# Raw projections, a shorter choice of experts and weights in halves at the layer ends of a two-layer encoder

## What is computed

```python
h = rms_norm(x, attn_norm_w[l])
proj = h @ w_in[l]                       # 1024 x 2700
a_q, a_k, a_v, b_z, b_xbc, b_dt, c_q, c_k, c_v = split(proj)
y_a = windowed attention with sinks (6 heads, 2 key heads)
y_b = bidirectional Mamba-2 block (conv of 5 taps, silu, softplus(dt), norm)
y_c = differential attention (4 heads x 2 maps), norm per head
x = x + concat(y_a, y_b, y_c) @ w_out[l]
h = rms_norm(x, ffn_norm_w[l])
# choice: best of 4 groups, best 2 of its 8 experts
out = sum over 32 experts of weight * ((silu(h @ w_gate) * (h @ w_up)) @ w_down)
x = x + out
```

## Time and profile before

| | |
|---|---|
| median of 3 runs | 1249.18 us (1249.11 to 1250.32) |
| profiled execution | 1250.82 us, span 1249.0 us |
| TensorE busy | 957.4 us (77%) |
| VectorE busy | 397.6 us (32%) |
| ScalarE busy | 187.2 us (15%) |
| mean granted TensorE clock | 0.896 of 2.4 GHz |
| HBM read | 433.65 MB, 348 GB/s over the span |
| chain that ended last | PE 42%, DMA 40%, DVE 9%, issue 5% |

### The profile page before, as it was taken

The page is one execution under the profiler, slowest core; times in us unless marked ns, Lnnn a source line. Parts: engine busy times, 40 slices in busy tenths (PEclk is TensorE's granted clock), DMA queues, the critical chain, the costliest instruction groups (busy, mean ns, idle before and its releaser), DMA issues.

```text
span 1249.0 us, 26485 instructions
## 1 busy us (share of the span) xinstructions
PE 957.4 (77%) x11004; PEld 605.4 (48%) x11004; DVE 397.6 (32%) x1224; ACT 187.2 (15%) x528; POOL 8.8 (1%) x27
## 2 busy tenths in 40 slices
PE   6999979666668787796689999786666666666964
PEld 5767855333334453453377777443333333333432
DVE  4668453111112222131166684521111111111213
ACT  1245221000000100010013452110000000000001
POOL 2000000000000000000000000000000000000000
PEclk8999989888889998998799999898888888888978
DMA  9825159999999999899994243599999999999994
GB/s 342 336 99 203 68 187 426 425 425 426 427 426 425 426 425 425 344 426 425 412 400 164 102 169 122 209 425 427 426 425 428 426 427 426 425 426 425 426 426 184
DMA packets 45961, 436.62 MB, mean 350 GB/s; under 512 B 8064, under 2 KB 10112, under 8 KB 21248
## 3 DMA queue, kind: packets, MB, share of 16 engines
q1 hardware_dynamic: 45824, 434.72, 84.1%
HBM read 433.65 MB, written 1.05 MB: 348 GB/s over the span
## 4 chain that ended last, share of the span: by engine, by line
PE 42%; DMA 40%; DVE 9%; issue 5%; DVEq 2%; ACT 1%; ACTq 0%
DMA ring<-in_w_up 39%; PE ps L562 16%; PE ps L638 7%; PE ps L573 4%; PE ps L761 3%; PE ps L650 2%; PE ps L543 2%; PE ps L582 2%; PE ps L701 1%; DVEq L1085 1%; PE ps L740 1%; PE ps L723 1%; PE ps L655 1%; DVE nmx L1258 1%; PE ps L692 1%
## 5 line engine op out<-in xcount | busy, mean ns | idle before, releaser
L562 PE MATMUL ps<-ring,xg 128*32 128x256 f32 x4096 | 310.3, 469 | 193.1 <-DMA ring<-in_w_up 189.1
L562 PEld LDWEIGHTS ps<-ring,xg 128*32 128x32 f32 x4096 | 166.7, 134 | 320.7 <-issue 273.5
L1062 DVE SCALAR_TENSOR_TENSOR gu<-th,ps 128x128 f32<-128x128 f32 x72 | 20.7, 288 | 615.2 <-ACT th L872 615.2
L573 PE MATMUL ps<-ring,actT 128*32 128x256 f32 x2304 | 139.2, 382 | 15.7 <-issue 13.3
L573 PEld LDWEIGHTS ps<-ring,actT 128*32 128x32 f32 x2304 | 69.0, 109 | 76.8 <-DVE actT L1066 24.1
L638 PE MATMUL ps<-hT,ring 128*128 128x256 f32 x416 | 99.5, 400 | 2.6 <-DVE hT L1112 2.6
L872 ACT ACTIVATE th<-ps 128x128 f32<-128x128 f32 x72 | 20.0, 278 | 526.8 <-PE ps L562 526.8
L638 PEld LDWEIGHTS ps<-hT,ring 128*128 128x128 f32 x416 | 82.2, 201 | 17.3 <-issue 2.4
L582 PE MATMUL ps<-ysb,PwT 32*128 32x256 f32 x1024 | 73.3, 400 | 1.0 <-ACT ysb L876 1.0
L543 PE MATMUL ps<-xh,Pb 128*32 128x256 f32 x1024 | 69.3, 387 | 0.0
L761 PE MATMUL ps<-ring,hT 128*128 128x256 f32 x256 | 59.2, 390 | 1.4 <-ACT hT L984 1.4
(11 more groups left out here) (251 smaller groups left out, 775.4 us busy)
## 6 DMA issues: line engine op xcount, KB each, us to landing
ring<-in_w_gate SPq DMA_DIRECT2D x64, 2048.0 KB, 43.0
ring<-in_w_up SPq DMA_DIRECT2D x64, 2048.0 KB, 37.9
ring<-in_w_down SPq DMA_DIRECT2D x64, 2048.0 KB, 42.4
ring<-in_w_in SPq DMA_DIRECT2D x8, 2048.0 KB, 20.4
ring<-in_w_out SPq DMA_DIRECT2D x4, 2048.0 KB, 20.3
ring<-in_w_in SPq DMA_DIRECT2D x2, 1584.0 KB, 27.2
x<-in_x SPq DMA_DIRECT2D x1, 1024.0 KB, 5.1
out<-fin SPq DMA_DIRECT2D x2, 512.0 KB, 2.7
```

Source lines behind the costliest of these rows:

```text
L562: last = mm(b_gate[j * SLOTS:(j + 1) * SLOTS, 0:2 * GQ], tokens[:, k, :], ring[:, low:high + 1:high - low, o:o + GQ], start=(k == 0), stop ...
L573: last = mm(b_y[j * SLOTS:(j + 1) * SLOTS, 0:DQ], actT[:, c * SLOTS:(c + 1) * SLOTS], ring[:, slot, o:o + DQ], start=(c == 0), stop=(c == ...
```

## The change

- **First piece in two transfers.** Piece 0 of `w_in` comes as k = 0 to 3, with the semaphore `head_landed`, and k = 4 to 7, with the slot's.
- **Raw projections.** `hT` is the transposed x times the norm's weights only, evicted by ScalarE. The first projection waits for these copies; in layer 1 it runs on TensorE ahead of `rs`. The root goes in behind: VectorE evicts `xbc`, `cq`, `aq`, `ak` and `ck` times a row of roots (`root_row`), `dt` times the root per token, and ScalarE `vz` and `cv` with it as scale. `root` is a tensor of its own.
- **Order.** `ORDER` is laid anew.
- **Square sum in quarters.** `sq2` is replaced by `sa.0` to `sa.2` on ScalarE, one behind each `xc2`, and `sd` on VectorE for the last quarter; `rs2` adds the four.
- **Shorter choice.** In `lg` equality and tie key are one instruction per token half, the group mask is one product and sum, and `sel` comes from the last key. The differences for the weights move to `wt`, the count has a step `cnt` of its own, the ranks keep their plus one (`RANK0` starts at 1), `route` comes last, and `W` and `Pw` of expert 0 are made behind its tokens. Its places run behind its hidden.
- **Row halves at layer ends.** Experts 0 and 31 (`EDGES`) load `front` (k = 0 to 3 of gate and up) and `back` (k = 4 to 7) in place of gate and up, each as two transfers of 1 MB on one slot's semaphore. `hidden` multiplies front when it has landed, frees its slot with `front_mm`, then waits for back.

```diff
 RING, LATE, REACH = 8, 2, 7
+EDGES = (0, NE - 1)
+           + [(part, e) for e in range(NE) for part in (("front", "back", "down") if e in EDGES else ("gate", "up", "down"))])
...
 ORDER = """
+    sq xT.0 xT.1 xT.2 xT.3 rs xbc.0 xbc.1 par dt xbc.2 conv.0 conv.1 silu.0 silu.1 xbc.3
+    conv.2 aq.0 silu.2 conv.3 ak xbc.4 aS.0 conv.4 dta silu.3 aq.1 silu.4 xs.0 sc.0 aq.2 cum
+    cumT sc.1 xs.1 nm.0 sc.2 seg.0.0 seg.0.1 cb.0 aS.1 rows.0 xdt pT.0 row.0.0 nm.1 row.0.1 cb.1
...
+    row.4.0 row.4.1 nm.4 y.3 cq.0 seg.5.0 seg.5.1 row.5.0 row.5.1 y.4 cq.1 sc.5 pT.2 sc.6 pT.3 cS.0
+    y.5 sc.7 ybn oa.0 pT.4 nm.5 cv oa.1 pT.5 cS.1 yT.0 yT.1 oa.2 sc.8 nm.6 sc.9
+    pT.6 sc.10 outA.0 pT.7 nm.7 sc.11 od.0 outA.1 sc.12 nm.8 pT.8 sc.13 outA.2 od.1 pT.9 od.2
+    od.3 nm.9 outA.3 ycn cT outB.0 outB.1 outB.2 outB.3 xc2.0 sa.0 xc2.1 sa.1 xc2.2 sa.2 xc2.3
+    sd fT.0 fT.1 fT.2 fT.3 rs2 lg seed xn2 wt cnt rank ov route
 """
...
+                    if n == 0:
+                        sp_.dma_start(to[:, 0:HALF, :], src[:, 0:HALF, :]).then_inc(head_landed, 16)
+                        to, src = to[:, HALF:, :], src[:, HALF:, :]
...
+                    k0 = HALF * FF * (part == "back")
+                    for h, w in enumerate((w_gate, w_up)):
+                        src = w[li, n, :, :].rearrange("(p k) f -> p (k f)", k=KC)[:, k0:k0 + HALF * FF]
+                        sp_.dma_start(to[:, h * HALF * FF:(h + 1) * HALF * FF], src).then_inc(signal, 16)
...
+                elif part == "front":
+                    sp_.wait_ge(M["front_mm"], len(EDGES) * li + EDGES.index(n) + 1)
...
+                if e in EDGES:
+                    for half, part in enumerate(("front", "back")):
+                        slot, signal, count = chunk(li, part, e)
+                        both = ring[:, slot, :].rearrange("p (h n) -> p h n", h=2)
+                        pe.wait_ge(signal, count)
+                        for k in range(HALF):
+                            for j in range(NQ):
+                                o = k * FF + j * GQ
+                                last = mm(b_gate[j * SLOTS:(j + 1) * SLOTS, 0:2 * GQ], tokens[:, half * HALF + k, :],
+                                          both[:, :, o:o + GQ], start=(half + k == 0), stop=(half == 1 and k == HALF - 1))
+                        last.then_inc(S["hidden_mm" if half else "front_mm"], 1)
+                    return
...
+                steps = list(PE_STEPS)
+                if li > 0:
+                    at = steps.index(("rs",))
+                    steps[at:at + 2] = steps[at + 1], steps[at]
...
+                            k = 2 * s[1] + a
+                            last = A(hT[:, k, :], bank[:, a * SEQ:(a + 1) * SEQ], ACT.Copy, scale=colp[:, K_AN + k:K_AN + k + 1])
...
+                    elif kind in ("xbc", "cq", "aq", "ak", "ck"):
+                        dve.wait_ge(done["act"], nth(li, "act", ("rs",)))
...
+                        last = v.tensor_tensor(to, bank[:, 0:SEQ], root_row[:, :], ALU.mult)
...
+                            for t in range(TT):
+                                v.scalar_tensor_tensor(score[:, t, :], vals[:, t, :], top[:, t:t + 1], tie[:, 0:k], ALU.is_equal, ALU.mult)
...
+                        for t in range(TT):
+                            last = v.scalar_tensor_tensor(sel[:, t, :], ta[:, t, :], gs[:, 1, t:t + 1], oh[:, 0, t, :],
+                                                          ALU.is_equal, ALU.add)
...
-                pe.wait_ge(M["prep_ready"], 2 * first + 2)
-                places(M, Pw[0])
                 pe.wait_ge(done["dve"], nth(li, "dve", ("ov",)))
...
+                    if e == 0:
+                        pe.wait_ge(M["prep_ready"], 2 * first + 2)
+                        places(M, Pw[0])
```

246 lines of the change are left out of this document (123 added, 123 removed).

## The result

The changed kernel took 1242.06 us (median of 5 runs, 1237.95 to 1242.5), 0.9925 of the kernel before, with a 95% interval of 0.9903 to 0.9946. I take 0.9918 of 1249.2, so 1239: 10 us faster, where 21.7 were forecast and the range ended at 1237.5.

A forecast was written before the change was run, and what follows sets the result against it. The kernel was taken as a chain: TensorE in projections and heads, VectorE in the choice, then weight loads for the experts. Savings of 8.5 (layer 0) and 13.2 (layer 1), 21.7 us off 1249.2, gave 1227.5, range 1219.5 to 1237.5.

The forecast's parts named there:

- Head of layer 1: Start of layer 1: first projection no longer waits for the norm's root; 5.4 us saved at full clock, 2.3 at 1.2 GHz.
- Head of layer 0: Start of layer 0: first projection starts at 12.4 instead of 13.82; 1.4 us saved, up to 3.1.
- The stretch between: First projection to last heads: VectorE's new order makes TensorE wait 1.9 us more a layer, bounds 0 and 4.
- Rival 4: VectorE bounds the middle stretch, 16.9 us a layer: 1257.7 us, 3%; partly through, 5 a layer: 1234 to 1240, 5%.
- (a): Choice of experts: the square sum on VectorE leaves the path, saving 1.15 us a layer.
- (b): Choice of experts, logits to sel: fewer and merged small dependent steps save 1.6 us a layer.
- (c): Choice of experts, sel to first gather: weights leave the path, 1.95 us remain, 1.8 saved a layer.
- (d): Half of expert 0's hidden frees the first slot, at full clock: sel to restart 5.85 us against 11.1.
- Whatever the clock: Layer 0's restart follows the next layer's parameter load, at 176.7, saving 6.4 us at any clock.
- rival 1: TensorE's clock stays at half at layer 1's head, its gather and both ends: 13.5 us saved, 1235.5 us; 17%.
- Ends: Last expert of each layer: first weight halves multiplied while the second load; 2.4 and 2.2 us saved, bounds 0.3 and 3.0.
- A restart that is earlier by d ends the layer earlier by d: Weight stream after the first expert: any time gained at its restart reaches the layer's end in full.

The follow-up runs named there:

- e12: The changed kernel run again with no edit: 0.9911 of the kernel before.
- e1_order: The changed kernel with the attention key's eviction and the weights' division nm.5 moved back earlier in VectorE's order: 0.9948 of the kernel before, 1242.7 us.
- e2: The changed kernel with added 128-column idle matmuls on TensorE before the wait for sel and before expert 0's hidden: 1.0049 of the kernel before, 1255.3 us.
- e6: As e2, but each idle matmul has one column instead of 128: 1.0095 of the kernel before, 1261.1 us.
- e10: The changed kernel with idle matmuls at the choice, expert 0's tokens transposed before route, and the next layer's parameters loaded three weight pieces later: 0.9931, 1240.6 us.
- e11: The changed kernel with e10's choice and parameter loads, and the mixer as before the change: 0.9921 of the kernel before, 1239.3 us.

## Why the prediction was wrong, step by step

The direction was right and the size half as large. The mean of the two traces puts the missing 9.8 us at: mixers 6.7, choice 3.5, ends -0.4. The runs that leave out the mixer's edits put 4.2 of it there (+1.3 measured against -2.9).

**Head of layer 1: right.** Forecast 4.3 us less from transposes to first projection, and full clock in it. Measured 3.7 less (2.9 instead of 6.6), and the first projection at clock 1.0.

**Head of layer 0: right.** In the trace after the first projection began at 12.44. Its first matmuls still came at 1.2 GHz, 0.43 us apart, up to 14.9; it ended some 3.1 us sooner, the upper bound. In e12 it began at 12.69, kept the slow pace up to 17.6 and ended 1.7 us sooner.

**The stretch between: the step that failed, in sign for the part as a whole.** I put 1.9 us a layer with a bound of 4. In layer 1 the stretch from first projection to transposes went from 133.4 to 138.4 (136.7 in e12), although 1.7 us of slow clock at its head were gone: 6.7 and 5.0 us. Of these 4.0 are idle (8.2 against 4.2): the waits that my walk had at 0.7, 1.1 and 1.6 measured 1.9, 1.2 and 1.6, and 0.9 and 0.7 stand behind them where I had 0.6. About 0.5 is the root's broadcast, which moved in, and 1.7 in the trace after is what 3.4 us more at 1.2 GHz cost. So the walk named the places rightly and sized the first wait at a third. And its bound was made of waits only. e1_order shows that this is not enough: the waits can be taken away and the time comes back, 3.4 us a layer in its trace, as clock. In the nine traces with the new mixer's order as it was changed, the end of layer 0 to the transposes is 140.4 to 142.5 us, in the six with the old mixer 140.5 to 144.2: the head's gain is used up in full. In layer 0 the transposes came at 149.0 to 153.4 instead of 147.7 to 149.8. What the edits do to the total is +6.2 alone and +1.3 in the change, where I had -2.9. So the term that failed is this one, 1.9 us a layer where layer 1 lost 6.7 and 5.0. Rival 4 had the direction and a likely reason, the first convolution that starts 16 us behind the first projection instead of 6 (measured 17.6 and 7.0). In full, 16.9 us a layer, it was far too large; "partly through (5 a layer)", 1234 to 1240 with a chance of 5%, came nearest to what happened.

**Choice, (a) and (b): nearly right.** 2.75 forecast, 2.0 in layer 1 and 2.3 in layer 0 (transposes to the count 24.5 before, 22.2 after, and 20.5 in e12, where TensorE had its full clock up to there). One price was low: a pair of instructions for equality and key takes 0.41 us and not 0.35.

**(c): right.** 1.95 forecast from the end of sel to gather; 1.99 in layer 1 and in e12, 2.62 in layer 0 of the trace after, at the slow clock.

**(d): failed as a clock, nearly right as a sum.** "This idle mostly vanishes, so I expect full clock" was the faulty sentence. 1.1 to 2.8 us of idle ahead of sel and narrow matmuls behind it were left, and the clock was 0.50 for gather or for half of hidden in both layers of both traces: from the end of sel to restart 9.3 and 8.0 us (8.3 and 8.3 in e12) instead of 5.85. At full clock, with idle work that ended in time, it was 6.1. "Whatever the clock" in layer 0 was wrong too: at the slow clock the half hidden is later than the parameters. Layer 1 held a second slip, the route steps between gather and tokens on VectorE (1.52 us of wait instead of 1.06). Half of rival 1 came true (its sum of 13.5 us gives 1235.7, not 1235.5), but the head of layer 1 had its full clock, and the choice's whole part in the miss is 3.5 us.

**Ends: right, by another path.** 2.4 and 2.2 forecast; 1.8 and 1.7 in layer 1, in the trace after with the second half at 1.2 GHz and down released by VectorE, in e12 by its load, and in all traces restart to end of layer 1 is 434.7 to 436.4 us with halves and 436.8 to 438.0 without. In layer 0 it scatters from 438.2 to 443.9, and reaches 448 to 456 where code or the queue was in the way (e2, e6, e10, e11).

**"A restart that is earlier by d ends the layer earlier by d": held in layer 1, within 1 us; in layer 0 only where nothing else stands in the queue.** e10's and e11's 8 us are the exception.

What I had left out altogether is that parts are not independent: the halves are worth 3.4 alone, 6.6 beside the short choice (a difference within the noise) and 11.4 with the new mixer as well.
